# A hybrid mixer and MoE layer on one core: first transfers, conditioning product, gate product, head rows and end rewritten

## The reference, cut to what matters

```python
mod = silu(c) @ w_ada + b_ada                  # one row for the prompt, one for the sample
sh1, sc1, g1, sh2, sc2, g2 = split(mod, 6)
z = (x * (1 + sc1) + sh1) @ w_in + b_in        # 11 groups of 512 columns, and 16 gate columns
y = [gelu(r_g) * rglru(r_x), hgrn2(...) * silu(g_o), sigmoid(m_o) * mlstm(...)] @ w_out
x = layer_norm(ALPHA * x + g1 * y)
f = moe(x * (1 + sc2) + sh2)                   # 16 experts, the best two of one group
x = layer_norm(ALPHA * x + g2 * f)             # mean and variance over 1024 columns
```

## Time and profile before

| | us |
|---|---|
| median of 3 runs (777.57 to 777.61) | 777.58 |
| the profiled execution's own time | 776.95 |
| its span, first to last instruction | 775.2 |
| PE busy in the span | 703.2 (91%) |
| DVE busy | 577.0 (74%) |
| ACT busy | 432.2 (56%) |
| mean granted TensorE clock | 0.962 of 2.4 GHz |

### The profile page before, as it was taken

The page is one execution under the profiler, slowest core; times in us unless marked ns, Lnnn a source line. Parts: engine busy times, 40 slices in busy tenths (PEclk is TensorE's granted clock), DMA queues, the critical chain, the costliest instruction groups (busy, mean ns, idle before and its releaser), DMA issues.

```text
span 775.2 us, 12312 instructions
## 1 busy us (share of the span) xinstructions
PE 703.2 (91%) x4722; PEld 553.5 (71%) x4722; DVE 577.0 (74%) x834; ACT 432.2 (56%) x597; POOL 58.5 (8%) x90
## 2 busy tenths in 40 slices
PE   3699999799999989999996999999999999999870
PEld 1477998698778969884453877888888888788630
DVE  2549697667995344573596988998999998999675
ACT  1546867245124344761122368888888888888510
POOL 4050000000010000024000300000000000000400
PEclk9799999899999989999998899999999999999986
DMA  9995599989665650319704999999999999999521
GB/s 331 359 299 199 210 333 384 374 321 401 256 231 177 229 218 5 109 30 163 305 1 148 404 402 394 398 398 399 400 400 400 399 399 399 399 399 381 168 80 54
DMA packets 91507, 220.06 MB, mean 284 GB/s; under 512 B 3335, under 2 KB 3631, under 8 KB 91455
## 3 DMA queue, kind: packets, MB, share of 16 engines
q1 hardware_dynamic: 84512, 197.66, 68.2%
q0 software_dynamic: 6528, 21.56, 9.1%
q10 hardware_dynamic: 415, 0.14, 0.1%
HBM read 179.99 MB, written 39.36 MB: 283 GB/s over the span
## 4 chain that ended last, share of the span: by engine, by line
PE 68%; DVE 11%; DMA 9%; ACT 4%; issue 4%; POOL 2%; SPq 0%; DVEq 0%; ACTq 0%; POOLq 0%
PE ps L1128 65%; DMA ring<-in_w_ada 3%; DMA iota<-in_consts 3%; DMA arena<-in_w_up 2%; PE ps L1515 1%; DMA slot_rows<-arena,small 1%; PE ps L1534 1%; POOL slot_rows L729 1%; DMA ring<-in_w_gate 1%; ACT w_hi L1027 1%; DVE w_lo L1676 1%; ACT w_hi L803 1%; DVE small L1953 1%; DVE picked_rows L2211 1%; DVE arena L1957 1%
## 5 line engine op out<-in xcount | busy, mean ns | idle before, releaser
L2130 DVE TENSOR_TENSOR w_lo<-arena,w_hi 128x1024 fp32r<-128x1024 f32 x96 | 114.7, 1221 | 12.3 <-ACT w_hi L1027 11.5
L2130 DVE TENSOR_TENSOR w_lo<-ring,w_hi 128x1024 fp32r<-128x1024 f32 x96 | 114.8, 1221 | 9.3 <-ACT w_hi L1027 8.4
L1027 ACT ACTIVATE w_hi<-ring 128x1024 fp32r<-128x1024 f32 x96 | 100.5, 1063 | 21.7 <-PE ps L1128 18.9
L1027 ACT ACTIVATE w_hi<-arena 128x1024 fp32r<-128x1024 f32 x96 | 100.8, 1065 | 17.9 <-PE ps L1128 13.7
L1128 PE MATMUL ps<-h_hi,w_lo 128*128 128x384 f32 x288 | 103.6, 360 | 6.2 <-DVE w_lo L1676 4.7
L1128 PE MATMUL ps<-w_hi,slot_tokens_lo 128*128 128x512 f32 x256 | 102.6, 401 | 0.8 <-DVE w_lo L2130 0.8
L1128 PE MATMUL ps<-w_hi,slot_tokens_hi 128*128 128x512 f32 x256 | 100.2, 391 | 0.0
L1128 PE MATMUL ps<-w_lo,slot_tokens_hi 128*128 128x512 f32 x256 | 99.8, 390 | 0.0
L1128 PE MATMUL ps<-h_lo,w_hi 128*128 128x384 f32 x288 | 98.8, 343 | 0.0
L1128 PE MATMUL ps<-h_hi,w_hi 128*128 128x384 f32 x288 | 98.6, 342 | 0.0
L1676 DVE TENSOR_TENSOR w_lo<-ring,w_hi 128x1024 fp32r<-128x1024 f32 x44 | 53.7, 1225 | 30.1 <-ACT w_hi L803 29.0
(11 more groups left out here) (352 smaller groups left out, 1115.9 us busy)
## 6 DMA issues: line engine op xcount, KB each, us to landing
slot_rows<-arena SPq DMA_DIRECT2D x12, 2048.0 KB, 17.0
ring<-in_w_in SPq DMA_DIRECT2D x11, 2048.0 KB, 11.5
ring<-in_w_ada SPq DMA_DIRECT2D x10, 2048.0 KB, 10.1
ring<-in_w_gate SPq DMA_DIRECT2D x8, 2048.0 KB, 18.3
ring<-in_w_up SPq DMA_DIRECT2D x8, 2048.0 KB, 19.2
ring<-in_w_down SPq DMA_DIRECT2D x8, 2048.0 KB
arena<-in_w_gate SPq DMA_DIRECT2D x8, 2048.0 KB, 18.4
arena<-in_w_down SPq DMA_DIRECT2D x8, 2048.0 KB, 15.1
```

The source lines that it names most:

```text
L1027: act.activation(w_hi[:, at_ % 4, :], raw[:, q * QUARTER:(q + 1) * QUARTER], ACT.Copy).then_inc(S["hi_ready"], 1)
L2130: tt(w_lo[:, at_ % 4, :], raw[:, q * QUARTER:(q + 1) * QUARTER], w_hi[:, at_ % 4, :].bitcast(F32), ALU.subtract).then_inc(S["lo_dve"], 1)
```

## The change

The schedule: ada_row 2, ada_col 0, ada_col 2 and h 0 now stand ahead of all transposes of x; gates is split into two steps.

```diff
-    steps = [("cond",), ("ada_row", 0), ("rows",)] + [("xT", 0, half) for half in range(2)] + [("ada_row", 2)]
-    steps += [("xT", i, 0) for i in range(1, NT)] + [("ada_col", 0), ("ada_col", 2), ("h", 0)]
+    steps = [("cond",), ("ada_row", 0), ("rows",), ("ada_row", 2), ("ada_col", 0), ("ada_col", 2), ("h", 0)]
+    steps += [("xT", 0, half) for half in range(2)] + [("xT", i, 0) for i in range(1, NT)]
...
-    ... ("conv", 1), ("gates",), ("conv", 2)]
-    steps += [gq[0], ("lru_mm", 0), ...
+    ... ("conv", 1), ("gates", 0), ("conv", 2)]
+    steps += [gq[0], ("gates", 1), ("lru_mm", 0), ...
```

```diff
@@ sync
                     piece(n, ada_v[:, :, name * G:(name + 1) * G], KD)
+                    if n == 1:
+                        sp.dma_start(x_in[:, 0, :], a["x_prompt"][0])...
+                        sp.dma_start(x_in[:, 1:3, :], a["x_sample"][0]...)...
+                        sp.dma_start(pos_in, a["pos"]...)...
@@ gpsimd
-            pool.dma_start(x_in[:, 0, :], ...) and the two below it, and gate_w
...
+            pool.dma_start(gate_w, a["w_in"][0, :, GATE_OFF:D_IN]...)...
             pool.dma_start(w_router, ...)
```

```diff
-                    for r in range(2):
+                    for kk in range(4):
                         for j in range(4):
-                            k = 4 * r + j
-                            last = mm(bank[32 * j:32 * j + 32, :], silu_w[:, 2 * k:2 * k + 32], w[k], r == 0, r == 1)
+                            k, cols = 4 * (j % 2) + kk, slice(256 * (j // 2), 256 * (j // 2) + 256)
+                            last = mm(bank[32 * j:32 * j + 32, 0:256], silu_w[:, 2 * k:2 * k + 32], w[k][:, cols], kk == 0, kk == 3)
...
-                    for c in range(4):
-                        last = mm(bank[:, 2 * c:2 * c + 2], ada_rows[:, b, c * P:(c + 1) * P], stream_sel)
+                    for x in range(2):
+                        last = mm(bank[:, 4 * x:4 * x + 4], ada_rows[:, b, x * P:(x + 1) * P], group_sel)
```

```diff
+                    if job[1] == 0:
+                        pe.wait_ge(S["gate_w_in"], 16)
+                        for r in range(2):
+                            for j in range(4):
+                                k = 4 * r + j
+                                last = mm(bank[32 * j:32 * j + 16, 0:T], gate_w[:, k, :], hT[:, k, :], r == 0, r == 1)
+                    else:
+                        for y in range(2):
+                            for d in range(2):
+                                last = mm(bank[at_:at_ + H, 0:T], ident_blocks[:, c0:c0 + H], gate_sums)
```

```diff
+                    step(ts(max_parts, zero_tile[:, 0:T], 0.0, None, ALU.mult))
...
+                    step(dve.tensor_copy(max_hi, MR))
+                    step(tt(max_parts[64:64 + HR, :], MR, max_hi.bitcast(F32), ALU.subtract))
+                    step(dve.tensor_copy(max_parts[0:HR, :], max_hi.bitcast(F32)), "m_rows")
...
-                    mm(ps[:, 3, 0:T], ident[r, 32 * d + h:...].broadcast_to([H, P]), MR[r, :])
+                    mm(ps[:, 3, 0:T], row_sel[0:64 + HR, 4 * d + h:...].broadcast_to([64 + HR, P]), max_parts[0:64 + HR, :])
```

```diff
             over = expert_pass(0)
             with act.If(over > P):
...
+            with act.Else():
+                first_picked()
+                out_rows_sb(NE - 1, NPAIR - 1, 1, True)
+            act.activation(rstd, eps, ACT.Sqrt)
             for i in range(NT):
                 act.wait_ge(S["ln_var"], NT + i + 1)
-                act.activation(rstd, mv_stats[:, 13:14], ACT.Sqrt, bias=eps)...
+                act.activation(PICK[:, 1, i, :], X1[:, i, :], ACT.Square, bias=row_mean[...], accum_out=row_sq[...])...
+                act.activation(row_rstd[...], row_sq[...], ACT.Sqrt, bias=eps, scale=1.0 / D)...
@@ vector
+            def mixed_rows(i):
+                for half, bank in enumerate(MIX_BANKS[i]):
+                    dve.wait_ge(S["mixed"], 2 * i + half + 1)
+                    step(tt(y[:, cols], ps[:, bank, :], g2_b[:, min(i, 1), cols], ALU.mult))
+                step(stt(X1[:, i, :], X1[:, i, :], 1.0, y, ALU.mult, ALU.add, accum_out=row_mean[:, i:i + 1]))
+                step(ts(row_mean[...], row_mean[...], -1.0 / D, None, ALU.mult), "ln_var")
+            def result(i):
+                dve.wait_ge(S["ln_std"], NT + 2 * i + 2)
+                step(stt(x, x, row_mean[...], ln_b[:, 2, :], ALU.add, ALU.mult))
+                step(dve.reciprocal(row_rstd[...], row_rstd[...]))
+                step(stt(x, x, row_rstd[...], ln_b[:, 3, :], ALU.mult, ALU.add), "out_tile")
+            mixed_rows(0)
+            mixed_rows(1)
+            result(0)
+            mixed_rows(2)
+            result(1)
+            result(2)
```

More of the change, by code:

```diff
@@ L853, in _ @@
                     act.wait_ge(S["rows_zeroed"], 1)
-                    for y in range(2):
+                    if job[1] == 0:
+                        act.activation(gate_sums, bank[:, 0:T], ACT.Identity).then_inc(S["z_taken"], 1)
+                    for y in range(2 * job[1]):
                         for d in range(2):
@@ L1242, in _ @@
                         pe.wait_ge(S["pos_added"], 1)
+                    if i == 1 and half == 1:
+                        pe.wait_ge(S["pos_added"], 2)
                     for k in range(4):
@@ L1707, in _ @@
                     modulated(job[1])
+                    if job[1] == 0:
+                        dve.wait_ge(S["x_in"], 32)
+                        dve.wait_ge(S["pos_in"], 16)
+                        for half in range(2):
+                            cols = slice(512 * half, 512 * half + 512)
+                            step(tt(x_in[:, 1:3, cols], x_in[:, 1:3, cols], pos_in[:, :, cols], ALU.add), "pos_added")
                 elif kind == "tile":
@@ L1827, in _ @@
                 elif kind == "rows1":
-                    taken_by_act(("gates",))
+                    taken_by_act(("gates", 1))
                     dve.wait_ge(S["gate_rows"], 3)
@@ L1947, in _ @@
             step(stt(chunk(YM, H - 1), ps[:, 2, 0:T], colsA[:, A_MLG + H - 1:A_MLG + H], chunk(MO, H - 1), ALU.mult, ALU.mult), "ym_done")
-            def norm(i, v, n, last="dve"):
-                x = X1[:, i, :]
-                for half in range(2):
-                    step(dve.bn_stats(mv_stats[:, 6 * half:6 * half + 6], x[:, half * 512:(half + 1) * 512]))
-                step(dve.bn_aggr(mv_stats[:, 12:14], mv_stats[:, 0:12]), "ln_var")
-                dve.wait_ge(S["ln_std"], n + 1)
-                step(dve.reciprocal(rstd, rstd))
-                step(stt(x, x, mv_stats[:, 12:13], ln_b[:, v, :], ALU.subtract, ALU.mult))
-                step(stt(x, x, rstd, ln_b[:, v + 1, :], ALU.mult, ALU.add), last)
             def with_cols(dst, src, cols):
@@ L2199, in _ @@
             dve.wait_ge(S["g2_in"], 16 * 2)
-            for i in range(NT):
-                s = min(i, 1)
-                y = PICK[:, 0, i, :]
-                if i == 0:
-                    dve.wait_ge(S["picked_scaled"], 1)
-                    step(stt(y, PICK[:, 1, i, :], pick_e[:, 1, i:i + 1], y, ALU.mult, ALU.add))
-                    step(tt(y, y, g2_b[:, s, :], ALU.mult))
-                    step(tt(X1[:, i, :], X1[:, i, :], y, ALU.add))
+            dve.wait_ge(S["picked_scaled"], 1)
+            first = PICK[:, 0, 0, :]
+            step(stt(first, PICK[:, 1, 0, :], pick_e[:, 1, 0:1], first, ALU.mult, ALU.add))
+            step(tt(first, first, g2_b[:, 0, :], ALU.mult))
+            step(tt(X1[:, 0, :], X1[:, 0, :], first, ALU.add))
+            def mixed_rows(i):
+                y = PICK[:, 0, i, :]
                 for half, bank in enumerate(MIX_BANKS[i]):
```

98 lines of the change are left out of this document (62 added, 36 removed).

## The result

The changed kernel takes 752.88 us (median of 4 runs, 751.41 to 754.24) against 777.6 for the kernel before in the same job: a ratio of 0.9688, interval 0.9672 to 0.9705, 24.7 us faster. The forecast was 762.9, range 757.0 to 769.5. The direction was right; the time lies 4 us under the range, and 10 us under the forecast. A second job gave 753.14 (ratio 0.9692, 0.9663 to 0.9720).

The account below looks back on a forecast made before the run. Transfer bytes bound the start, PE the mixer and expert passes, a chain the end. Terms −3.8 −0.8 −2.0 +1.5 −2.5 −3.3 −3.8 = −14.7 from the median 777.58 give 762.9 us, range 757.0 to 769.5.

Parts of the forecast that it names:

- start: First 30 us: transfers in order on one queue let the first w_hi start at 26.4, not 30.24; −3.8 us.
- ada_col: Conditioning product: four turning products fewer save 0.4 to 0.42 each; −0.8 for 1 and 3, −2.5 for 5 to 10.
- gates: Gate product near 60 us: 3.3 us of records removed, 1.3 returns as PE's wait for w_lo; −2.0.
- rounded maxima: Three more DVE instructions ahead of the w_lo at 104.86 lengthen PE's wait near 112; +1.5 us.
- head rows: Two records of 0.83 us together become one fp32r product of 0.28, counted six times; −3.3 us.
- expert passes: Register read moves into the passes, covered by slack on ACT, DVE and PE; 0, or +0.8 us if uncovered.
- end: After the experts: PE's mixing starts as before, ACT and DVE start earlier, last result at 764.3 against 768.08; −3.8 us.
- rival 5: gate_w lands late, with the 20.6 us small transfer time: 9.3 us lost, 772.2; chance 0.02.
- rival 2: Weight loads exposed in ada_row, 10 x 4 x 0.13 = 5.2 us back: 768.1; chance 0.07.
- rival 1: DVE bounds the mixer: gates and ada_col 5 to 10 bring 0, head rows half; 769.0; chance 0.12.
- rival 3: PE's clock stays up at the end, −6.9 us there instead of −3.8: 759.8; chance 0.10.
- Rival 4: New PE waits lower the clock, up to 3.4 us per stretch; chances: one or two 0.07, about four 0.02, more 0.04.

Follow-up runs that it names:

- al_before: Kernel before with 24 short fp32 products of zeros (96 instructions) ahead of PE's first wait for constants: ratio 0.9946, 4.2 us faster than the kernel before.
- u_cols: Changed kernel with only the conditioning product undone (512-column ada_rows, four turning products), no padding: ratio 0.9881, 15.0 us slower than the changed kernel.
- al_cols: Changed kernel with the old conditioning product and 44 zero products (176 instructions) ahead on PE: ratio 0.9779, 7.1 us over the changed kernel.
- al_gates: Changed kernel with the old one-step gate product and 44 zero products (176 instructions) ahead on PE: ratio 0.9727, 3.0 us over the changed kernel.
- al_after64: Changed kernel with only 64 zero products (256 instructions) added ahead on PE: ratio 0.9726, 3.0 us over the changed kernel.

## Why the forecast fell short, step by step

| term | forecast | measured |
|---|---|---|
| start | −3.8 | −3.5 in the traces (29.34 for 32.81); −2.3 by the undone run |
| ada_col | −3.3 | −3.5 in the traces (8 x 0.44); −4.1 to −7.1 by the runs, with other losses in it |
| gates | −2.0 | −2.1 in the trace; 0 to −3.0 by the run |
| rounded maxima | +1.5 | +1.2 (waits of 1.31 and 0.66 for 0.36, less the 0.44 that the ada_col ahead of them saves) |
| head rows | −3.3 | −5.1 in the traces, 0.84 each; with the maxima −5.4 by the run |
| expert passes | 0 | 0 |
| end | −3.8 | −9.0 in the traces; −8.2 by the undone run |
| where blocks of instructions end | not in the sum | −2.4 in the traces (5.7 of "issue" for 8.1 ahead of the end); −4.2 by al_before, with the clock behind it |

The terms by the traces add up to −24.4, and the two traces differ by 24.3. They can be cut at products that both kernels have, the first of the mixer, a head row, the first and the last of the experts; the kernel before, then the changed one:

```profile
32.81 0.66 PE L1128 MATMUL ps<-h_hi,w_lo 128*128 128x384 f32 x1 [4.38 <-DVE w_lo L1676]
...
441.93 0.47 PE L1128 MATMUL ps<-w_hi,slot_tokens_lo 128*128 128x512 f32 x1
...
736.05 0.40 PE L1128 MATMUL ps<-w_hi,expert_act_hi 128*128 128x512 f32 x1
```

```profile
29.34 0.66 PE L1155 MATMUL ps<-h_hi,w_lo 128*128 128x384 f32 x1 [4.50 <-DVE w_lo L1716]
...
262.43 0.42 PE L1155 MATMUL ps<-max_parts,row_sel 100*128 100x384 f32 x1
...
426.57 0.48 PE L1155 MATMUL ps<-w_hi,slot_tokens_lo 128*128 128x512 f32 x1
```

| from | to | before | after | difference | forecast |
|---|---|---|---|---|---|
| start of the span | first product of the mixer | 32.81 | 29.34 | −3.5 | −3.8 |
| there | first head row (272.72, 262.43) | 239.91 | 233.09 | −6.8 | −3.8 |
| there | first expert product | 169.21 | 164.14 | −5.1 | −3.3 |
| there | last expert product | 294.12 | 294.15 | 0.0 | 0 |
| there | end of the span | 39.15 | 30.18 | −9.0 | −3.8 |

More than half of what the forecast lacks is in the last row.

**Start: right.** ada 0 came at 9.9 (forecast 9), the position add began at 21.5 (20.9), the first w_hi at 26.85 (26.4). Order on one queue did what the bytes at 379 GB/s said. gate_w was in time, and rival 5 is out. What I called half clock for the first ada_row was inferred from its 3.64 being twice 1.92: the granted clock of that stretch reads 1.00 in the trace, before and after the change.

**Conditioning product: right.** ada_row kept its 1.9 us with twice the weight loads, so rival 2 is out, and so is the rule of the Trainium skill that I set beside it, at least for these calls ("TensorE: Matmul & The Clock Gate", section "The mechanism"): here loads into the same rows do lie beside running matmuls. Start-to-start of an ada_col fell from 0.81 to 0.37 (120.97 to 121.34):

```profile
120.97 0.51 PE L1155 MATMUL ps<-small,extra 128*128 128x4 f32 x4
121.34 0.42 PE L1155 MATMUL ps<-h_hi,w_lo 128*128 128x384 f32 x1
```

0.44 for each of eight is 3.5, against the forecast's 3.3. The four that it put at nothing are at nothing in the trace of u_cols, which has the old turning products: its first product of the mixer starts at 29.34 too (ada_col 0 and 2), it goes from the ada_col near 101 to the next product in 1.87 against 1.82, and from number 11 to the next head row in 2.67 against 2.65, since a shorter ada_col is followed by a longer wait there (1.31 against 0.92, 2.15 against 1.71). What al_cols shows beyond 3.5 is thus not turning work; 2.8 of it is its longer end.

**Gates and maxima: right.** PE waited for w_lo as forecast (0.83 at 58.88, forecast 1.3), and rival 1 is out: DVE's density (22.26 of 24) did not take the savings back. The undone run alone would not show the gates' 2.1, since al_gates is level with its control.

**Head rows: mis-sized.** The step "0.83 together become 0.28" looked at the start of the records and of the next one. It left out that the product behind the old records started 0.32 before its own follower (305.50 to 305.82), now 0.23, and that the one ahead was held 0.31 (304.35 to 304.66), now 0.15. The price was 0.84, not 0.55; six times 0.3 is 1.8 of the shortfall.

**End: the step that failed outright, 5.2 of the 10 missing.** "PE's compare-and-branch is 5.49 us from 734.9, so PE's mixing starts as now", and "moving only the read cannot shorten PE's part". The read and the branch run on the sequencer, ahead of the array, which still works off its queue. Placed ahead of the down product, the read (0.48 and the register work behind it) is out of the way, and the branch starts while expert products still run: 718.7, with the last product starting at 720.72. Its own length was 3.99 us too, against 5.06 to 5.49 in the traces where the read stands behind; with the read ahead it was 3.67 to 5.10, so its length is not fixed by the read, and what sets it stays open. The rule from the Trainium skill ("Runtime: NRT & Kernel Launch", section "Instruction fetch mechanics") that a taken branch forces a fetch is not contradicted: 3.7 to 5.5 us stay on the sequencer, though no run shows that a fetch is what takes them. What I concluded from it, that the idle time therefore stays on the array, was wrong. The second part was rival 3, to which I gave 0.10: with 1.78 us idle in place of 4.15 the granted clock stayed up, and four mixing records took 1.95 instead of 3.75. The forecast's own bound for it, −6.9, still falls short of the 9.0 in the traces and lies within the interval of the 8.2. An early PE is worth something only with the new order of DVE and ACT: in pad_b64, the kernel before with 32 instructions ahead, the idle happens to be 2.21 and the four mixing records take 1.96, and the time from the last expert product to the end is 38.95, against 39.15.

**Not in the forecast at all:** the idles for "issue" in the runs of short products. They were in the profile of before (12.3 us in nine waits, 4.15 of them behind the branch), and I read them as a property of the work. They are a property of how many instructions stand ahead. At the place that the changed kernel happens to have, the kernel before takes 774.1, not 777.8 in that job, so of the 24.7 us some 4 are luck. The edits as such bring about 20 against the changed kernel, and 17 against its padded control al_after64; the paddings cannot say it more closely. Both are above the forecast's 14.7: in the traces its terms lack 5.2 at the end and 1.8 at the head rows.

**Clock.** Rival 4 (new waits lower the clock) is out in the changed kernel: the mean granted clock is 0.967 against 0.962. But its mechanism is what makes a badly placed idle dear: in u_cols 6.4 us more of "issue" in the page's sum (12.1 against 5.7) went with 15.0 in time, 3.5 of it the turning products.

## What to carry to other kernels

Read the "issue" waits of PE before anything else is costed: inside runs of very short products they belong to the place of the instructions, and any edit moves them. Before a few microseconds are credited to an edit, repeat kernel and edit with some dozen harmless instructions ahead; undoing one part alone here gave 15.0 us for a part whose own work is 3.5 in the traces. A register read that a branch needs belongs ahead of the last long stretch of work, since the sequencer can then take the branch while the array still works; here that was 3.5 us behind the last expert product.

## What the runs showed of the hardware

- PE's instructions come in blocks, and a run of products that start 10 ns apart (192 in 1.83 us) can outrun them: the idle at ada_row 6, 2.8 to 4.9 us, moves by exactly the instructions put ahead and returns to the same product with 256 more. The Trainium skill ("Runtime: NRT & Kernel Launch", section "Instruction fetch mechanics") states a block of 256 instructions, with which this agrees, and calls the cost of its end mostly hidden, with which the 3.2 us here do not agree.
- 32 instructions of pure waiting ahead of the first instruction, in 7 us in which PE is idle anyway, changed the time by +3.5 in one kernel and −2.3 in the other.
- Two waits ahead of PE were packed into one instruction: 64 in the source were 32 in the trace.
- PE's branch took 3.67 to 5.49 us on the sequencer in the 20 traces, and in 18 of them the first product behind it started 0.13 to 0.21 us after its end. The same PE instructions gave 3.99 and 3.91 in one kernel and 4.61 and 4.79 in another that differs only on DVE.
- A head row as an fp32 product with 4 weight rows cost 0.84 us more than as one fp32r product with 100, of which 0.25 lies at its edges and not in its own two records. Type and rows changed together; which of the two costs it was not separated.
